# Score matmuls of two heads issued one per step, instead of in adjacent pairs, in the attention stage of a decoder step

## The reference

```python
def diff_attention(q, k, v, q_pos, lam):
    s = jnp.einsum('bqhcd,bkhcd->bhcqk', q, k).astype(jnp.float32) * (DH_DIFF ** -0.5)
    causal = jnp.arange(k.shape[1])[None, :] <= q_pos[:, None]
    p = jax.nn.softmax(jnp.where(causal, s, -jnp.inf), axis=-1)
    a = p[:, :, 0] - lam * p[:, :, 1]
    return jnp.einsum('bhqk,bkhe->bqhe', a.astype(v.dtype), v)

def dsa_attention(q, k, v, q_idx, k_idx, w_idx, q_pos, k_sel):
    ...
    score = jnp.einsum('bqhk,bqh->bqk', jax.nn.relu(dots), w_idx.astype(jnp.float32))
    score = jnp.where(causal[None], score, -jnp.inf)
    _, idx = lax.top_k(score, k_sel)
    ...
```

## Time and profile before

| | us |
|---|---|
| median of three executions | 1279.35 |
| their range | 1274.09 to 1280.02 |
| the profiled execution (one of the three) | 1274.09 |
| its span in the profile | 1272.3 |
| TensorE busy, share of the span | 1074.9, 84% |
| VectorE busy | 498.3, 39% |
| ScalarE busy | 234.9, 18% |
| HBM traffic over the span | 251 GB/s |

### The profile page before, as it was taken

One profiled execution on the slowest core, in us unless ns is written; L12 is line 12 of the kernel. 1 busy time (PEld: TensorE's weight loads), 2 busy tenths in 40 slices (PEclk: granted clock), 3 DMA queues, 4 the chain that ended last, 5 costly groups with the idle time before them and its releaser, 6 DMA issues. The chain is left out here.

```text
span 1272.3 us, 16258 instructions
## 1 busy us (share of the span) xinstructions
PE 1074.9 (84%) x6061; PEld 558.7 (44%) x6061; DVE 498.3 (39%) x1291; ACT 234.9 (18%) x506; POOL 184.8 (15%) x178
## 2 busy tenths in 40 slices
PE   4989999878699999899899969999777778877873
PEld 2544444434344455533245545554444344443442
DVE  3325985995567768532233442311110011111110
ACT  2102221110133334330102421111111110111000
POOL 1012201220000000100200012232222222212211
PEclk9989999989899999999999969999999998999998
DMA  5141122015354533369909448999999999999991
GB/s 178 32 144 35 61 92 83 26 67 196 102 190 139 185 110 126 126 254 345 317 15 420 163 149 349 400 396 397 398 402 403 398 403 403 405 404 406 406 391 50
DMA packets 77126, 304.15 MB, mean 239 GB/s; under 512 B 22406, under 2 KB 22406, under 8 KB 64758
## 3 DMA queue, kind: packets, MB, share of 16 engines
q1 hardware_dynamic: 61622, 273.47, 56.0%
q0 software_dynamic: 9824, 16.98, 4.7%
q10 hardware_dynamic: 5600, 12.65, 2.7%
HBM read 290.03 MB, written 29.66 MB: 251 GB/s over the span
## 5 line engine op out<-in xcount | busy, mean ns | idle before, releaser
L368 PE MATMUL p_z<-k_w,k_xT 128*128 128x512 f32 (+2 forms) x528 | 214.2, 562 | 5.9 <-DMA k_w<-in_w_in 5.3
L368 PEld LDWEIGHTS p_z<-k_w,k_xT 128*128 128x128 f32 (+1 forms) x528 | 94.9, 193 | 113.2 <-issue 107.5
L776 PE MATMUL a_G<-k_w,k_xT 128*128 128x512 f32 x256 | 132.0, 640 | 2.5 <-ACT k_x L834 2.5
L1915 DVE TENSOR_TENSOR e_den<-e_sig,e_G 128x256 f32<-128x256 f32 x32 | 13.5, 421 | 276.6 <-ACT e_sig L1820 276.6
L1825 ACT ACTIVATE e_y<-e_Y,x_share 64x512 f32<-64x512 f32 x64 | 43.7, 683 | 314.0 <-PE e_Y L1728 305.1
L1946 POOL DMA_INDIRECT out_y_p<-e_y,x_table x32 | 45.0, 1407 | 199.7 <-ACT e_y L1825 143.8
L776 PEld LDWEIGHTS a_G<-k_w,k_xT 128*128 128x128 f32 x256 | 45.6, 199 | 49.6 <-issue 45.7
L1920 DVE TENSOR_TENSOR e_a<-e_den,e_U 128x256 f32<-128x256 f32 x32 | 13.5, 421 | 126.7 <-PE e_U L1716 126.7
L1120 PE MATMUL g_ring<-k_w,k_oT 128*128 128x512 f32 x128 | 61.0, 624 | 0.0
L134 POOL DMA_INDIRECT k_rows<-token_rows,x_table x32 | 31.2, 976 | 188.2 <-PE e_TX L1710 162.6
L1716 PE MATMUL e_G<-k_oT,e_xT 128*64 128x256 f32 x352 | 45.3, 411 | 12.8 <-DMA k_oT<-in_w_gate 12.8
(11 more groups left out here) (341 smaller groups left out, 1464.8 us busy)
## 6 DMA issues: line engine op xcount, KB each, us to landing
k_w<-in_w_in SPq DMA_DIRECT2D x11, 2048.0 KB, 7.7
k_w<-in_w_gate SPq DMA_DIRECT2D x11, 2048.0 KB, 45.0
k_w<-in_w_up SPq DMA_DIRECT2D x11, 2048.0 KB, 45.0
k_xT<-in_w_down SPq DMA_DIRECT2D x11, 2048.0 KB, 45.5
k_oT<-in_w_gate SPq DMA_DIRECT2D x11, 2048.0 KB, 43.3
k_side<-in_w_up SPq DMA_DIRECT2D x11, 2048.0 KB, 45.2
x_page<-in_w_down SPq DMA_DIRECT2D x11, 2048.0 KB, 45.2
x_merged<-in_w_gate SPq DMA_DIRECT2D x10, 2048.0 KB, 43.9
```

The source lines that it names most:

```text
L368: last = nc.tensor.matmul(z[u % 3][0:p, 0:WIDTH[k]], s.xT[:, j, 128 * i:128 * i + p], s.w[:, c % 2, j, 0:WIDTH[k]], start=j == 0, stop=j = ...
L776: last = nc.tensor.matmul(G[u % 2][:], s.xT[:, j, 128 * i:128 * i + 128], s.w[:, q % 2, j, :], start=j == 0, stop=j == KD - 1)
L1915: v.tensor_tensor(den[:], sig[:], G[j][:, 0:HW], ALU.mult).then_inc(chain, 1)
```

## The change

The scores of one unit are issued in each step, where before the scores of two units were issued in each even step. The pair loop over r is gone; r is now the first of the 64 rows. Step n waits for `max_ready` of n - 1 (the maximum of the unit two before, which used the same bank) and from step 2 on, where before it waited for n.

```diff
             for n in range(STEPS):
-                if n < UN and n % 2 == 0:
+                if n < UN:
                     t, kind, h = A_UNITS[n]
                     kq, kk, _ = KQV[kind]
-                    if n:
-                        pe.wait_ge(max_ready, n)
-                    for r in range(2):
-                        nc.tensor.matmul(S[r][:, 0:128 * (t + 1)], s.T[kq][64 * r:64 * r + 64, h // 2, 128 * t:128 * t + 128],
-                                         s.T[kk][64 * r:64 * r + 64, h // 2, 0:128 * (t + 1)], start=True, stop=True).then_inc(scored, 1)
+                    r = 64 * (h % 2)
+                    if n >= 2:
+                        pe.wait_ge(max_ready, n - 1)
+                    nc.tensor.matmul(S[n % 2][:, 0:128 * (t + 1)], s.T[kq][r:r + 64, h // 2, 128 * t:128 * t + 128],
+                                     s.T[kk][r:r + 64, h // 2, 0:128 * (t + 1)], start=True, stop=True).then_inc(scored, 1)
                 gates(n)
```

## The result

The changed kernel takes 1291.23 us (median of 7, 1286.45 to 1294.77), the kernel before 1277.65 (median of 7 beside it, 1274.04 to 1280.02). The ratio is 1.0105, with a 95% interval of 1.0082 to 1.0129: 10.5 to 16.5 us slower, where 14.0 were predicted. (The changed kernel was run more often than these seven times; all executions on record lie between 1283.65 and 1295.90.) The span of the profiled executions grew by 16.3 us, from 1272.3 to 1288.6 (each 1.8 less than the execution's own time).

A forecast was written before the change was run, and what follows sets the result against it. TensorE was taken to bound the attention stage, its delays reaching the end. 27.8 - 2.8 - 2.0 - 5.8 - 1.8 - 1.7 + 0.3 = +14.0 us on the median 1279.35 gave 1293; range 1284 to 1302.

The forecast's parts named there:

- The bound and the end: Attention stage: TensorE is the bound, and a us gained or lost there comes out at the end as a us.
- The row of waits at the start: From 856 us on: nine waits for expert weights like the 45.95 us shown, each followed by a few us of matmul.
- The inserted matmuls, +27.8: Attention stage: 32 score matmuls standing alone each cost a whole pair's time plus borders, 0.55 to 1.19 us; +27.8 us on TensorE.
- The row of the projection stage: Projection stage: a lone index product of 64 rows and 256 columns takes 0.63 us, as much as a whole score pair.
- The pull-ahead of weight loads: Borders of full- and half-height matmuls: a rival had loads hidden, inserted matmuls costing columns only, +4.9 us, 1284; chance 6%.
- The idle load engine: Ahead of the score loads at 331.68: idle 0.76 us with a_G running, read as nothing being pulled ahead.
- The stall, -2.8 and -2.0: Wait for the fifth key page: five inserted matmuls fit into idle time, -2.8; earlier release at its end, -2.0.
- the other maxima, -5.8: TensorE's waits for maxima in 7 places outside the stall disappear, as it wants the maximum one unit earlier; -5.8 us.
- a_on, -1.8: TensorE's waits ahead of turning the outputs shrink by the score matmul now beside them, or to nothing; -1.8 us.
- The new wait, +0.3: Step 17: its scores are now issued in the step itself, so a_G waits for ScalarE's copy; +0.3 us, at most 2.05.
- The clock, -1.7: At 361 to 364: 3.4 us of half clock disappear, one wait ahead being shorter and another gone; -1.7 us, bounds 0 and 1.7.
- the stretch at 422: Clock fall where a_G waits 2.05 us for ScalarE's copy: left as it was, scores being issued just ahead in both versions.

The follow-up runs named there:

- e4: The kernel before, with SyncE reading each key page's number just ahead of that page's load instead of all 32 first; 1263.64 us, ratio 0.9884.
- e3: The kernel before, with the score pair kept but issued behind the step's two gate matmuls, except in steps 34 and 50; 1277.41 us, ratio 1.0001.
- e5: The changed kernel, with each key page's number read just ahead of that page's load; 1281.28 us, ratio 1.0031 to the kernel before.
- e2: The changed kernel, but step n waits for the maxima of all n units before, as the pairs did; 1298.61 us, ratio 1.0170 to the kernel before.
- e9: The kernel before, with the score pair issued behind the gate matmuls only in seven steps where TensorE had waited; 1271.28 us, ratio 0.9964.
- e7: The kernel before, with single score matmuls in the first query tile only (units 0 to 15) and pairs after it; 1275.67 us, ratio 0.9989.

## Why the prediction was right, by its steps

*The bound and the end.* TensorE bounds the attention stage, and a us there is a us at the end: the last column of the table, and e4, whose gain of 13.8 us in the stage is a gain of 13.3 between the medians. The row of waits at the start is misread in one number: the chain before has eight long waits for weights from 856 us on (36.33 to 46.99 us), not nine; nothing rests on it. VectorE's waits cost nothing of their own: 36.2 us before, 42.1 in e3 with an unchanged time, 51.2 after, and TensorE's matmuls, waits and clock make up the whole difference (below).

*The inserted matmuls, +27.8.* From start to start one alone takes 0.62 and 1.05 us for 256 and 512 columns in the profile after, where its pair took 0.63 and 1.06. To get the sum from the traces, I take each stage without TensorE's idle time and count what is done at half clock at half its length: 192.2 us of work before, 219.3 after, so 27.1 for the 32 inserted; 192.3 in e4 and 219.4 in e5, again 27.1. The row of the projection stage in the earlier trace rows had been enough to tell this. The pull-ahead of weight loads that the Trainium skill describes (TensorE: Matmul & The Clock Gate, "The mechanism" in Part 3) does not hide the border of full-height and half-height matmuls here: a_O to a_S is 0.49 us (400.93 to 401.42), as in the earlier trace rows, where a_O to a_G is 0.40. The idle load engine in the earlier trace rows, which the prediction set against the rule, is weaker evidence than it reads: that load also stood behind a wait for a maximum, ready 0.64 us before (the a_nb at 330.89 ends at 331.04). The load at 402.04, which waits for nothing, shows the same without it.

*The stall, -2.8 and -2.0, and the other maxima, -5.8.* Together with the stall's idle time they should have taken 10.6 to 11.3 us; the waits for maxima fell by 10.7. In e2 the looser wait is worth 6.3 us of TensorE's idle time. e5 against e4 shows that the stall hid a part of the cost.

*a_on, -1.8.* From 4.0, counting the stage's last, to 2.2.

*The new wait, +0.3.* It did not come at step 17: ScalarE's copy cost the same 2.5 us in both. A wait of 0.41 came elsewhere, at the a_T of 359.43.

*The clock, -1.7, was wrong in sum.* The half clock at 361 is gone, as forecast, but the reason given, shorter waits, is not shown and may be luck: e4 has both waits at that place, as long as before, and ran at full clock behind them (a_G takes 1.82 us, 348.62 to 350.44):

```profile
346.61 0.66 PE L764 MATMUL a_T<-k_c,a_on 128*128 128x128 f32 x4 [1.46 <-DVE a_on L904]
348.19 0.49 PE L790 MATMUL a_S<-t_Tks,t_Tqs 64*128 64x128 f32 x4 [0.93 <-DVE a_nb L942]
348.62 1.98 PE L777 MATMUL a_G<-k_w,k_xT 128*128 128x512 f32 x4
350.44 0.27 PE L745 MATMUL a_T<-k_c,a_prob 128*128 128x128 f32 x1
```

Behind the stall the half clock even fell from 10 to 3.4 us. But the stretch at 422, which I had left as it was, grew from 3.4 to 10.2 us. The lost time is half of what TensorE was busy in such stretches: (4.5 + 3.4 + 3.4) / 2 = 5.7 before, (3.4 + 9.4) / 2 = 6.4 after. In place of a gain there is +0.7 for stall and clock together, where -1.7 and a loss of about 0.7 inside the -2.0 were counted, so 1.7 more than predicted.

The stage then comes to 27.8 - 10.7 - 1.8 + 0.4 + 0.7 = +16.4, against 16.0 measured in the profiled executions and 13.6 between the medians. By the traces' own sums it is 27.1 of work, less 12.3 of idle time, plus 1.2 of half clock (0.5 of it at the two ends of the stage, which the list above leaves out): +16.0.

So the mechanism is the one forecast, and the size of its two large terms too. That 1291.23 lies within 2 us of 1293 is in part luck: the clock was off by 1.7 us, and single executions of the changed kernel lie 8 us and more apart.

## What to carry to other kernels

Two float32 matmuls of 64 rows that use different rows of the array cost the time of one when they are issued next to each other (1.06 us at 512 columns), and the time of two (1.05 each) as soon as a full-height matmul stands between. Count what a move does on the engine that is the bound before counting whose waits it ends: here it ended 12 us of waits for 27 us of matmuls. A wait can also be shortened by moving what is behind it ahead of it, but in these runs that paid only where no other chain starts from what is delayed by that (e3 against e9).

## What the runs showed that I had not expected

The half clock behind one and the same wait is not a constant. Behind the 2.05 us at 422 it was on for 3.4 us before and for 10.2 after (2.06 us of waiting there), and e9 ran at full clock behind the same wait:

```profile
419.46 1.98 PE L776 MATMUL a_G<-k_w,k_xT 128*128 128x512 f32 x4 [2.05 <-ACT k_x L838]
```

e7 had half clock behind two waits, of 1.20 and 1.33 us, that the kernel before has too (at 460.82 and 516.71) and passed at full clock. In the attention stage it came to between 6.7 and 30.7 us over these runs. A term of the clock can be given for a sum of such stretches with a bound of a few us, and not place by place.
